# Second norm at three edges: its sum of squares put together from sums gathered in the product, its tiles done one by one, and the next product's first three output tiles together

## The reference

```python
        x = x + (1.0 + g_m) * rms_norm(y, norm_mix_post[i])
        h = rms_norm(x, norm_ffn_pre[i]) * (1.0 + sc_f) + sh_f
        y = conv_ffn(h, ffn_w_gate[i], ffn_w_up[i], ffn_conv_w[i], ffn_conv_b[i], ffn_w_down[i])
        x = x + (1.0 + g_f) * rms_norm(y, norm_ffn_post[i])
```

## Time and profile before

| | us |
|---|---|
| median of 3 runs | 2508.35 (2505.41 to 2512.46) |
| the profiled execution: its time | 2508.84 |
| its span, first to last instruction | 2507.0 |
| PE busy | 2406.8 |
| mean granted TensorE clock | 0.982 of full speed |

### The profile page before, as it was taken

How to read it: one execution, slowest core, us unless ns; L and a number is a source line. 1 busy time by engine, 2 the same in 40 slices (tenths; PEclk the granted TensorE clock), 3 DMA queues, 4 the chain that set the end, 5 groups by cost and what they waited for, 6 DMA issues and landing times. The chain is left out here.

```text
span 2507.0 us, 34255 instructions
## 1 busy us (share of the span) xinstructions
PE 2406.8 (96%) x13948; PEld 1951.7 (78%) x13948; DVE 1731.7 (69%) x2700; ACT 677.4 (27%) x1248; POOL 196.8 (8%) x169
## 2 busy tenths in 40 slices
PE   8997879999999999999999999999999999999997
PEld 6885768887788888787765578888888888888886
DVE  7663666866888875738878777666666886666653
ACT  3212444012111110423577712222202112322200
POOL 0001341100000002000121010000010001000001
PEclk9998989999999999999999999999999999999999
DMA  5220002331233354422210073323463452223341
GB/s 186 76 74 0 3 19 76 111 118 51 84 96 98 97 186 146 152 68 76 76 35 1 2 247 98 109 93 101 149 239 107 160 214 72 93 93 101 122 143 63
DMA packets 70333, 252.82 MB, mean 101 GB/s; under 512 B 7808, under 2 KB 8096, under 8 KB 69664
## 3 DMA queue, kind: packets, MB, share of 16 engines
q1 hardware_dynamic: 69888, 250.08, 29.9%
q10 hardware_dynamic: 288, 0.54, 0.1%
HBM read 248.50 MB, written 2.10 MB: 100 GB/s over the span
## 5 line engine op out<-in xcount | busy, mean ns | idle before, releaser
L393 PE MATMUL psum<-rounded_n,rounded_high 128*128 128x512 f32 x1856 | 737.9, 398 | 4.4 <-DVE rounded_n_low L547 1.8
L395 PE MATMUL psum<-rounded_n,rounded_ring 128*128 128x512 f32 x1856 | 725.3, 391 | 0.0
L394 PE MATMUL psum<-rounded_n_low,rounded_high 128*128 128x512 f32 x1856 | 725.1, 391 | 0.0
L347 DVE TENSOR_TENSOR rounded_ring<-ring,rounded_high 128x1024 fp32r<-128x1024 f32 (+1 forms) x360 | 446.4, 1240 | 43.4 <-ACT rounded_high L330 31.4
L393 PEld LDWEIGHTS psum<-rounded_n,rounded_high 128*128 128x128 f32 x1856 | 350.4, 189 | 84.9 <-issue 7.5
L394 PEld LDWEIGHTS psum<-rounded_n_low,rounded_high 128*128 128x128 f32 x1856 | 350.4, 189 | 77.4 <-issue 5.5
L395 PEld LDWEIGHTS psum<-rounded_n,rounded_ring 128*128 128x128 f32 x1856 | 350.0, 189 | 73.7
L345 DVE CAST rounded_high<-ring 128x1024 fp32r<-128x1024 f32 (+1 forms) x347 | 236.6, 682 | 189.1 <-PE psum L395 182.2
L393 PE MATMUL psum<-rounded_arena,rounded_high 128*128 128x512 f32 x720 | 280.9, 390 | 4.4 <-DVE rounded_ring L347 4.4
L394 PE MATMUL psum<-rounded_arena,rounded_high 128*128 128x512 f32 x720 | 280.6, 390 | 0.0
L395 PE MATMUL psum<-rounded_arena,rounded_ring 128*128 128x512 f32 x720 | 280.6, 390 | 0.0
(11 more groups left out here) (478 smaller groups left out, 3030.4 us busy)
## 6 DMA issues: line engine op xcount, KB each, us to landing
ring<-in_w_up SPq DMA_DIRECT2D x132, 512.0 KB, 3.5
ring<-in_w_down SPq DMA_DIRECT2D x48, 512.0 KB, 3.5
n_low<-in_mod_w SPq DMA_DIRECT2D x48, 512.0 KB, 5.6
arena<-in_mod_w SPq DMA_DIRECT2D x48, 512.0 KB, 5.4
ring<-in_w_ab_in SPq DMA_DIRECT2D x37, 512.0 KB, 3.5
ring<-in_w_mix_in SPq DMA_DIRECT2D x31, 512.0 KB, 3.5
ring<-in_w_sc_in SPq DMA_DIRECT2D x24, 512.0 KB, 5.4
ring<-in_w_down SPq DMA_DIRECT2D x24, 384.0 KB, 3.1
```

The source lines that it names most:

```text
L347: nc.vector.tensor_tensor(self.rounded(raw), raw, self.rounded(high), ALU.subtract).then_inc(self.weights_split, 1)
L393: self.nc.tensor.matmul(out, w_high, x_high, start=first, stop=False)
L394: self.nc.tensor.matmul(out, w_high, x_low, start=False, stop=False)
L395: return self.nc.tensor.matmul(out, w_low, x_high, start=False, stop=last)
```

## The change

At the three edges (after ab_out, down_1 and sc_out) `joined_edge` takes the place of `edge`. The state after the edge is h + r·g·y, with r the first norm's inverse root per token. Its sum of squares is the old state's, kept in `roots[:, 3, :]`, plus r·(r·S1 + 2·S2), with S1 the sum of (g·y)² and S2 the sum of g·y·h. Both are gathered in the product: per output tile one more square with a scale on ScalarE, one more product on VectorE (`crosses`, one buffer), two more additions on GpSimd. The gain g must be there: `finish` is called for the first eight rows after the second output tile, and in ab_out and down_1 the first three output tiles are gathered together at the third; in sc_out, whose gain is known, one by one. At the edge the eight squares of the new state are gone, PE sums S1 and S2, five small VectorE operations put the sum together, and from the third tile on VectorE scales, adds, norms and takes the low part tile by tile. `lead` is 3 in up_1, up_2 and sc_in. `double_edge`, ahead of ab_in, writes the sum to `roots[:, 3, :]` instead of `roots[:, 1, :]`. The last edge and down_2's product are as before, but for the place of `finish`.

```diff
+def joined_edge(k, name, before, first_gain, gain, shift, then, y):
...
+    def sums_of(i):
+        return k.psum[:, SUMS[i], :].rearrange("p (c x) -> p c x", x=P)[:, :, 0:1]
...
+    def add_up(i, total, first):
+        for c in range(TT):
+            end = nc.tensor.matmul(k.psum[:, SUMS[i], c * P:(c + 1) * P], total[:, c * P:(c + 1) * P], ones,
+                                   start=first and c == 0,
+                                   stop=not first and c == TT - 1)
+        return end
+    def tensor(pe):
+        pe.wait_ge(added, KT - 1)
+        add_up(0, k.sum_sq, True)
+        pe.wait_ge(squared, KT)
+        add_up(0, k.squares[:, last, :], False).then_inc(summed, 1)
+        pe.wait_ge(gain_added, KT - 1)
+        add_up(1, k.rstd, True)
+        pe.wait_ge(gain_squared, KT)
+        add_up(1, k.scaled_squares[:, last, :], False)
+        spread_root(pe, 0)
+        pe.wait_ge(cross_added, KT - 1)
+        add_up(2, k.cross_sum, True)
+        pe.wait_ge(crossed, KT)
+        add_up(2, k.crosses, False).then_inc(products_summed, 1)
+        pe.wait_ge(out, KT)
+        keep_busy(k, pe, 6)
+        spread_root(pe, 1)
+        keep_busy(k, pe, 9)
+    def scalar(act):
+        act.wait_ge(summed, 1)
+        nc.scalar.activation(k.roots[:, 0, :].unsqueeze(2), sums_of(0), ACT.Sqrt, bias=k.const("eps"), scale=1.0 / D
+                             ).then_inc(rooted, 1)
+        act.wait_ge(total, 1)
+        nc.scalar.activation(k.roots[:, 1, :], k.roots[:, 3, :], ACT.Sqrt, bias=k.const("eps"), scale=1.0 / D
+                             ).then_inc(rooted, 1)
+        for j in range(KT):
+            act.wait_ge(scaled, j + 1)
+            nc.scalar.activation(k.rounded(k.n[:, j, :]), k.n_low[:, j, :], ACT.Identity,
+                                 bias=shift[:, j:j + 1]).then_inc(shifted, 1)
+    def vector(dve):
+        link = Link(dve, steps)
+        def grow(j):
+            link(nc.vector.scalar_tensor_tensor(y[:, j, :], y[:, j, :], first_gain[:, j:j + 1],
+                                                k.psum[:, SPREAD[0], :], ALU.mult, ALU.mult))
+        def renew(j):
+            link(nc.vector.tensor_tensor(k.h[:, j, :], k.h[:, j, :], y[:, j, :], ALU.add))
+        def norm(j):
+            nc.vector.scalar_tensor_tensor(k.n_low[:, j, :], k.h[:, j, :], gain[:, j:j + 1],
+                                           k.psum[:, SPREAD[1], :], ALU.mult, ALU.mult).then_inc(scaled, 1)
+        def low_part(j):
+            dve.wait_ge(shifted, j + 1)
+            low = k.n_low[:, j, :]
+            nc.vector.scalar_tensor_tensor(k.rounded(low), low, shift[:, j:j + 1], k.rounded(k.n[:, j, :]),
+                                           ALU.add, ALU.subtract).then_inc(done, 1)
+        k.split_weights(dve, then, 0)
+        dve.wait_ge(rooted, 1)
+        nc.vector.reciprocal(k.roots[:, 0, :], k.roots[:, 0, :]).then_inc(inverted, 1)
+        dve.wait_ge(inverted, 1)
+        dve.wait_ge(spread, 1)
+        dve.wait_ge(out, KT)
+        grow(0)
+        renew(0)
+        dve.wait_ge(products_summed, 1)
+        r, a, h_squares = (k.roots[:, i, :].unsqueeze(2) for i in (0, 2, 3))
+        link(nc.vector.tensor_tensor(a, r, sums_of(1), ALU.mult))
+        link(nc.vector.scalar_tensor_tensor(a, sums_of(2), 2.0, a, ALU.mult, ALU.add))
+        link(nc.vector.tensor_tensor(a, a, r, ALU.mult))
+        link(nc.vector.tensor_tensor(h_squares, h_squares, a, ALU.add))
+        nc.vector.tensor_scalar(h_squares, h_squares, 0.0, None, ALU.max).then_inc(total, 1)
+        grow(1)
+        dve.wait_ge(rooted, 2)
+        nc.vector.reciprocal(k.roots[:, 1, :], k.roots[:, 1, :]).then_inc(inverted, 1)
+        renew(1)
+        dve.wait_ge(spread, 2)
+        norm(0)
+        norm(1)
+        low_part(0)
+        for j in range(2, KT):
+            grow(j)
+            renew(j)
+            norm(j)
+            low_part(j - 1)
+        low_part(KT - 1)
+    return Stage(tensor=tensor, scalar=scalar, vector=vector, done=done)
...
-    def finish(self, dve):
+    def finish(self, dve, first, last):
         k, nc = self.k, self.k.nc
-        link = Link(dve, self.summed)
-        dve.wait_ge(self.used, self.n)
-        a, b = self.first, self.first + self.n
+        if self.link is None:
+            self.link = Link(dve, self.summed)
+        link, a, b = self.link, self.first + first, self.first + last
+        dve.wait_ge(self.used, last)
         link(nc.vector.tensor_tensor(k.mod_cols[:, a:b], k.mod_cols[:, a:b], k.vec("mod_b")[:, a:b], ALU.add))
         for part in range(a // KT, b // KT):
...
-            k.product(pe, name, k.normed, T, out, inputs_ready=before.signals["done"], lead=2)
+            k.product(pe, name, k.normed, T, out, inputs_ready=before.signals["done"], lead=3)
...
+    LATE = 2 if mod is not None else 0
+    def ready(j):
+        return [] if gain is None or j < LATE else range(LATE + 1) if j == LATE else [j]
...
             nc.scalar.copy(y[:, j, :], k.psum[:, j % PRODUCT_BANKS, :]).then_inc(out, 1)
+            for i in ready(j):
+                if i == 0:
+                    act.wait_ge(gain_made.summed, 2 if gain_made is mod else 3)
+                act.wait_ge(out, i + 1)
+                if i >= 2:
+                    act.wait_ge(gain_added, i - 1)
+                nc.scalar.activation(k.scaled_squares[:, i % 2, :], y[:, i, :], ACT.Square, scale=gain[:, i:i + 1]
+                                     ).then_inc(gain_squared, 1)
     def pool(pool):
-        add_squares(k, pool, squared, added, tiles=KT - 1)
+        if gain is None:
+            add_squares(k, pool, squared, added, tiles=KT - 1)
+            return
+        for j in range(KT - 1):
+            pool.wait_ge(squared, j + 1)
+            if j == 0:
+                nc.gpsimd.tensor_copy(k.sum_sq[:], k.squares[:, 0, :]).then_inc(added, 1)
+            else:
+                pool.wait_ge(added, j)
+                nc.gpsimd.tensor_tensor(k.sum_sq[:], k.sum_sq[:], k.squares[:, j % 2, :], ALU.add).then_inc(added, 1)
+            for i in ready(j):
+                pool.wait_ge(gain_squared, i + 1)
+                if i == 0:
+                    nc.gpsimd.tensor_copy(k.rstd, k.scaled_squares[:, 0, :]).then_inc(gain_added, 1)
+                else:
+                    pool.wait_ge(gain_added, i)
+                    nc.gpsimd.tensor_tensor(k.rstd, k.rstd, k.scaled_squares[:, i % 2, :], ALU.add
+                                            ).then_inc(gain_added, 1)
+                pool.wait_ge(crossed, i + 1)
+                if i == 0:
+                    nc.gpsimd.tensor_copy(k.cross_sum, k.crosses).then_inc(cross_added, 1)
+                else:
+                    pool.wait_ge(cross_added, i)
+                    nc.gpsimd.tensor_tensor(k.cross_sum, k.cross_sum, k.crosses, ALU.add).then_inc(cross_added, 1)
...
             k.split_weights(dve, name, j)
             if mod is not None and j >= 0:
                 mod.sums(dve, j)
-        if mod is not None:
-            mod.finish(dve)
-
-    return Stage(sync, tensor, scalar, vector, pool, squared=squared, added=added, out=out)
+                if gain is not None and j == 1:
+                    mod.finish(dve, 0, KT)
+                if j == KT - 2:
+                    mod.finish(dve, KT if gain is not None else 0, mod.n)
+            for i in ready(j):
+                dve.wait_ge(out, i + 1)
+                if i >= 1:
+                    dve.wait_ge(cross_added, i)
+                nc.vector.scalar_tensor_tensor(k.crosses, y[:, i, :], gain[:, i:i + 1], k.h[:, i, :],
+                                               ALU.mult, ALU.mult).then_inc(crossed, 1)
...
+        k.crosses, k.cross_sum = k.scratch[:, 4, :], k.scratch[:, 5, :]
...
+        norm_1 = joined_edge(k, "ffn_norm_1", mixed, mod_part(k, 0, 2), mod_part(k, 0, 4), mod_part(k, 0, 3), "up_1", k.n)
```

More of the change, by code:

```diff
@@ L3277, in tensor @@
     def tensor(pe):
-        k.product(pe, "sc_in", k.normed, T, out, inputs_ready=before.signals["done"], lead=2)
+        k.product(pe, "sc_in", k.normed, T, out, inputs_ready=before.signals["done"], lead=3)
     def scalar(act):
@@ L3457, in build @@
             (k.z[:, XR + kk, :], k.z[:, GR + kk, :]) if kk < KT
[L3458 to L3459 removed]
+            else (k.z[:, NQT + kk - KT, :], k.ab_low[:, kk - KT, :])), k.n, mod, gain=mod_part(k, 0, 2), gain_made=mod)
+        norm_1 = joined_edge(k, "ffn_norm_1", mixed, mod_part(k, 0, 2), mod_part(k, 0, 4), mod_part(k, 0, 3), "up_1", k.n)
         up_1 = ffn_up(k, 1, norm_1)
         mod = Modulation(k, "down_1", 40, 24, 4, *modulation_room(k.n_low), after=mod)
[L3462 to L3463 removed]
+        down_1 = plain_product(k, "down_1", k.hidden, k.n, mod, up_1, gain=mod_part(k, 0, 5), gain_made=mod)
+        norm_2 = joined_edge(k, "sc_norm", down_1, mod_part(k, 0, 5), mod_part(k, 1, 1), mod_part(k, 1, 0), "sc_in", k.n)
         mod = Modulation(k, "sc_in", 64, 24, 1, *modulation_room(k.hid_high[:, KT + 1:2 * KT + 1, :]), after=mod)
```

(2 more changed lines are left out.)

38 lines of the change are left out of this document (27 added, 11 removed).

## The result

The changed kernel takes 2535.28 us (median of 3 runs, 2535.11 to 2540.77) against 2508.35; the ratio is 1.0116, 95% interval 1.0101 to 1.0131. It is slower, as forecast (2523), but by 27 us and not 15: 0.3 us beyond the range's upper end of 2535.

A forecast was written before the change was run, and what follows sets the result against it. TensorE, busy 2406.8 of 2507.0 us, was taken as the bound. Edges -1.1, ab_out +11.8, down_1 +2.8 and clock +1.4 summed to +14.9, 2523 us on the median; range 2505 to 2535, likeliest 2516 to 2531 (0.50).

The forecast's parts named there:

- edges: Three edges: 0.25 us later at up_1 and up_2, 1.6 gained at sc_in; -1.1, with 0.5 either way each.
- ab_out, waits: TensorE waiting in ab_out: 5.2 us at the third step plus 6.6 over steps 4 to 6; +11.8, between 4.1 and 18.7.
- down_1, wait: In down_1, TensorE waits once for the fourth tile's weight split: 2.8 us taken, between +1.8 and +4.6.
- clock: Granted clock falls after long TensorE waits in ab_out, up_1, up_2: one fall taken, 1.4 us; bounds 0 and 4.2.
- I take 5.2: ab_out's third step: TensorE waits for the split before the fifth output tile's product, at least 4.1, up to 7.0 us.
- The three later steps: ab_out's steps 4 to 6: 2.2 us each, from product tile and GpSimd passes; 6.6 together, bounds 2.1 and 11.7.
- there is no slack: ab_out's steps 4 to 6: VectorE's loop 10.85 against TensorE's step of 10.87, so a product tile adds 0.66 us.
- 2 if GpSimd is late at the end: sc_out: GpSimd's three passes plus holds take some 4.9 per 5.4 us; no cost taken, 2 if late.
- Rival 3: Every GpSimd pass holds VectorE and each long wait lowers the clock: +26, 2534 us; chance 0.12.
- Rival 1: Product waits at lower bounds, GpSimd's passes falling under the DMA wait: +4.8, 2513 us, no change; chance 0.28.
- Rival 2: Gathering hidden and up_1's and up_2's fourth-tile weights ready in time, so edges keep 3.5 us each: 2498 us; chance 0.10.
- the upper bound that the forecast drew from it: By the shared-port rule alone every GpSimd pass would hold a busy VectorE, putting ab_out at its upper bound, 18.7 us.

The follow-up runs named there:

- a4: The changed kernel with 15 small matmuls into an idle bank ahead of the fourth output tile of up_1 and up_2: 2528.60 us, ratio 1.0084.
- c1: The changed kernel with small matmuls filling TensorE's four idle waits, in ab_out, down_1, up_1 and up_2: 2525.48 us, ratio 1.0081.
- b2: The changed kernel without GpSimd's two added passes per output tile, so the sums lack tiles 1 to 6: 2517.75 us, ratio 1.0044.
- after: The changed kernel itself, as profiled, against the kernel before the change: 2535.28 us, ratio 1.0116.
- a3: The changed kernel with VectorE splitting the fourth weight tile ahead of the first two taps in up_1 and up_2: 2522.96 us, ratio 1.0065.
- a1: The changed kernel with the old edges and two output tiles together, only the gathering left: 2537.88 us, ratio 1.0122.
- d1: Kernel before plus spread gathering, placed ahead of the step's own square in down_1, joined edges 2 and 3, up_2's early split: 2504.74 us, ratio 0.9988.

## Why the prediction had the sign and missed the size

The sum of +14.9 against what the segments and windows show:

| term | forecast | measured |
|---|---|---|
| edges | -1.1 | +0.1 |
| ab_out, waits | +11.8 | +13.5 |
| down_1, wait | +2.8 | +4.1 |
| clock | +1.4 | +8.3 |
| sum | +14.9 | +26.0 |

- **The clock** is the step that failed, and 6.9 of the 11.1 missing. "I take one fall, 1.4; bounds 0 and 4.2" took the fall behind the earlier trace rows as the size, and one in three waits as the count. There were four falls, one behind each of the waits of 6.98, 3.89, 3.57 and 3.57 us, and they lasted up to 5.4 us and not 2.8, so even the upper bound was half of it. The row used was a wait of 4.0; waits of 5.2, 3.7 and 3.7 stood in the same text, and nothing in the rows spoke for counting only one of them. Nor was down_1's wait, forecast at 2.8 us, counted among them. a4 and c1 show this term.
- **ab_out's waits.** "I take 5.2" at the third step: 6.98, the upper bound of 7.0, since both later cross products and the split were held. The three later steps: 5.3 of wait by the timeline, some 6.2 in all (each distance grew by 0.25 to 0.3 more than its wait, and the sum had no term for that), against 6.6. That these agree is in part luck: the sum put 0.66 of its 2.2 per step to the product tile itself, since "there is no slack", and b2 shows that this costs nothing; the held instructions took more than their share.
- **down_1**: 3.89 and 0.2 behind it against 2.8, between the bounds; the same three products, two held (1.70 and 1.67), and the subtraction of the split behind them too (1.90 at 1870.52, where the same one took 0.96 at 1850.11).
- **The edges.** At edge 1 +0.3 (forecast +0.25) and at edge 2 -1.5 (-1.6); both chains were right to 0.3 us at every joint measured. Edge 3: +1.3 in place of +0.25, where the text named "2 if GpSimd is late at the end" and took nothing. Late was VectorE, held by GpSimd's passes: the last cross starts at A+2.23 behind a split of 2.18 and the reciprocal at A+4.75, where they stand at A+1.11 and A+3.64 at edge 1, and at edge 3 of b2.
- Rival 3 (each pass holds VectorE, each wait lowers the clock; 2534) had the third step right and that every long wait is followed by a fall. That its total of +26 fits is luck: its sum has 18.7 for ab_out, 5 more than measured, and 4.2 for the clock, 4 less. The forecast's 11.8 was nearer in ab_out. Rival 1 fell with after's own steps and b2: the added passes do not fall under the DMA wait. Rival 2's point on the fourth tile held in a3, at 2.5 and 1.4 and not 3.5 each.
- The forecast weighed a rule of the Trainium skill (SBUF — State Buffer, section "SBUF: two separate sides"): the engine that starts first holds the shared ports for its whole instruction, and the other blocks. The traces agree in who pays and nearly in how much: VectorE's instructions grew by 0.9 to 1.1 us, the rest of the pass under way less 0.1 to 0.2. They do not bear out the upper bound that the forecast drew from it, since in ab_out not every pass met an instruction of VectorE that TensorE waited for.

What stays open: why the clock fell behind a wait of 2.2 us in c1 and not behind 2.27 and 2.61 in after; how the third step's wait divides between holds and the single buffer; and ab_out's first square, which lies up to 10 us apart between these variants (1451.35 in a4, 1461.54 in a1) with nothing edited ahead of it. The clock has a part in that (between 200 and 400 us its mean was 0.95 in a4 and 0.90 in a1), and why it differed is not known.

## What to carry to other kernels

- Where a change makes TensorE wait, price each wait twice: its own length, and a stretch at half clock behind it (here 2.9 to 5.4 us long behind waits of 3.57 to 7 us). If the wait can't go, small matmuls in it kept the second part away here at all four places, though in ab_out another fall then came behind the next wait.
- An idle engine isn't a free one. GpSimd was at 8%, but a pass that was under way when VectorE began an instruction took about 1 us from it, and in ab_out that reached TensorE. The same passes cost down_1 nothing once they were spread and queued ahead (d1, 104.72), and left sc_out at 38.08, though they made the edge behind it 1 us late. Ask in which product an addition stands, not how busy the engine is on the page.
- An edge whose norm started 8 us sooner gave 1.4 to 2.5 at its best: look first at what the next stage waits for behind it, and at what is queued in front of that.
